# A streaming encoder step: queries projected in transposed form, keys and values two tiles to a PSUM bank

## The reference, cut to what matters

```python
h = rms_norm(x, norm_mix_g)
z = h @ w_in
u_pool, q, k, v, gate_logits = jnp.split(z, IN_SPLITS, axis=-1)
q = rope_partial(q.reshape(B, T, N_HEADS, 2, HEAD_DIM), pos)   # rotates the first 16 of each 64 dims
k = rope_partial(k.reshape(B, T, N_HEADS, 2, HEAD_DIM), pos)
...
s = jnp.einsum('bqhmd,bkhmd->bhmqk', q, k) * ATTN_SCALE        # m: the two halves of a head
p = softmax(where(mask, s, -inf));  a = p[:, :, 0] - lam * p[:, :, 1]
attn = einsum('bhqk,bkhv->bqhv', a, v)
```

## Time and profile before

| | us |
|---|---|
| median of 3 runs | 845.22 |
| lowest, highest | 845.0, 848.85 |
| span of the profiled execution | 843.6 |
| PE busy | 821.1 |
| DVE busy | 588.7 |
| ACT busy | 512.7 |

### The profile page before, as it was taken

One profiled execution on the slowest core, in us unless ns is written; L12 is line 12 of the kernel. 1 busy time (PEld: TensorE's weight loads), 2 busy tenths in 40 slices (PEclk: granted clock), 3 DMA queues, 4 the chain that ended last, 5 costly groups with the idle time before them and its releaser, 6 DMA issues.

```text
span 843.6 us, 15839 instructions
## 1 busy us (share of the span) xinstructions
PE 821.1 (97%) x5378; PEld 748.1 (89%) x5378; DVE 588.7 (70%) x957; ACT 512.7 (61%) x935; POOL 87.6 (10%) x76
## 2 busy tenths in 40 slices
PE   8999999999999999999999999999999999999992
PEld 7999999999999999999999888888888888888881
DVE  6373332777677768467467126999989999989995
ACT  7343313666566656565525233488888887888884
POOL 0000000000000000000000001222223322223112
PEclk9999999999999999999999999999999999999996
DMA  9632213232133213332234746699999999999925
GB/s 274 139 103 83 67 44 95 82 109 75 36 104 107 59 54 108 102 101 75 79 123 157 270 177 204 236 371 372 380 377 374 368 368 367 364 368 367 351 70 193
DMA packets 135959, 163.54 MB, mean 194 GB/s; under 512 B 18599, under 2 KB 103719, under 8 KB 135914
## 3 DMA queue, kind: packets, MB, share of 16 engines
q1 hardware_dynamic: 129674, 149.53, 52.7%
q0 software_dynamic: 5952, 12.82, 5.4%
q10 hardware_dynamic: 288, 0.59, 0.2%
HBM read 151.61 MB, written 20.12 MB: 204 GB/s over the span
## 4 chain that ended last, share of the span: by engine, by line
PE 52%; DVE 3%; DMA 2%; issue 1%; ACT 1%; POOLq 0%; POOL 0%; ACTq 0%
PE ps L1748 15%; PE ps L1750 15%; PE ps L1749 15%; PE ps L2182 2%; PE ps L2094 1%; DMA xg<-sum_rows,idi 1%; PE ps L2101 1%; PE ps L2204 1%; DMA sum_rows<-yb,ydn 1%; PE ps L2086 0%; PE ps L2127 0%; PE ps L2128 0%; PE ps L2025 0%; DVE wl L1144 0%; PE ps L1953 0%
## 5 line engine op out<-in xcount | busy, mean ns | idle before, releaser
L1623 DVE TENSOR_TENSOR wl<-rawM,wh 128x1024 fp32r<-128x1024 f32 x189 | 223.9, 1220 | 14.3 <-ACT wh L980 12.4
L980 ACT ACTIVATE wh<-rawM 128x1024 fp32r<-128x1024 f32 x192 | 195.8, 1057 | 6.2 <-PE ps L1750 2.8
L1748 PE MATMUL ps<-hTh,wh 128*128 128x272 f32 (+2 forms) x448 | 131.0, 292 | 1.4 <-ACT qkv L804 1.0
L1750 PE MATMUL ps<-hTh,wl 128*128 128x272 f32 (+2 forms) x448 | 129.5, 289 | 0.0
L1749 PE MATMUL ps<-hTl,wh 128*128 128x272 f32 (+2 forms) x448 | 128.9, 288 | 0.0
L1748 PE MATMUL ps<-wh,xh 128*128 128x256 f32 (+1 forms) x384 | 124.3, 324 | 0.3 <-DVE xl L1669 0.3
L1750 PE MATMUL ps<-wh,xl 128*128 128x256 f32 (+1 forms) x384 | 121.7, 317 | 0.0
L1749 PE MATMUL ps<-wl,xh 128*128 128x256 f32 (+1 forms) x384 | 121.6, 317 | 0.0
L1748 PE MATMUL ps<-wh,hTh 128*128 128x384 f32 x256 | 90.0, 352 | 0.2 <-DVE mA L1254 0.2
L1748 PEld LDWEIGHTS ps<-hTh,wh 128*128 128x128 f32 x448 | 84.3, 188 | 3.0 <-ACT qkv L804 1.3
L1750 PE MATMUL ps<-wh,hTl 128*128 128x384 f32 x256 | 86.3, 337 | 0.0
(11 more groups left out here) (324 smaller groups left out, 1711.5 us busy)
## 6 DMA issues: line engine op xcount, KB each, us to landing
rawM<-in_w_expert_up SPq DMA_DIRECT2D x64, 512.0 KB, 9.2
rawM<-in_w_expert_down SPq DMA_DIRECT2D x64, 512.0 KB, 8.0
rawM<-in_w_expert_gate SPq DMA_DIRECT2D x64, 512.0 KB
rawA<-in_w_in SPq DMA_DIRECT2D x64, 192.0 KB, 3.0
rawA<-in_w_in SPq DMA_DIRECT2D x20, 512.0 KB, 5.3
rawA<-in_w_attn_branch SPq DMA_DIRECT2D x8, 512.0 KB, 3.5
rawA<-in_w_out SPq DMA_DIRECT2D x8, 512.0 KB, 4.2
x<-in_x_prompt SPq DMA_DIRECT2D x4, 512.0 KB, 6.7
```

What stands on the lines that cost most here:

```text
L980: nc.scalar.activation(wh[:, (c + 1) % S, :], rawM[:, slot, :], ACT.Copy).then_inc(m_hi, 1)
L1623: V.tensor_tensor(wl[:, sl, :], rawM[:, slot, :], wh[:, sl, :].bitcast(F32), ALU.subtract).then_inc(m_lo, 1)
L1748: T.matmul(out, sh, mh_, start=start, stop=False, **kw)
L1750: return T.matmul(out, sl, mh_, start=False, stop=stop, **kw)
```

## The change

Queries leave the token-row form. In each step they are now made by `queries(j, half, ...)`: 128 columns of weights are the stationary operand, and 272 tokens move past, twice, into banks 3 and 4: 6 matmuls of 272 columns. The result is transposed already. Keys and values (`keys_values`) keep the tile as stationary operand, with 256 columns moving; two tiles share a bank, so banks 0, 1 and 2 hold them. In steps 0 to 6 the queries come after the tiles and after the attention pieces that are tied to tile 4, in step 7 ahead of the tiles. `turn(g)` has 6 transposes instead of 11.

ACT copies three key and value banks (512, 512, 256 elements) and then, behind them, the queries (544 elements, `copy_queries`). The rotation of the queries is done in the transposed form by DVE: times a table of signed sines (`scale_queries`), times a table of cosines and a swap of partitions by STREAM_SHUFFLE (`swap_queries`), and an addition (`turn_queries`). They stand at three places of DVE's order. Then ACT rounds them (`qh`) and DVE takes `ql`, each in one instruction of 544. The key rotation is half as wide, and is moved ahead of the second query step. `clamp(g, 0)` is moved behind the splits of q and k; the split of v is behind it. The two tables (128 x 544 each) are loaded once, ahead of the first cached keys.

```diff
+            def copy_queries(h):
+
+                act.wait_ge(q_mm, h + 1)
+                if not (isinstance(h, int) and h == 0):
+                    act.wait_ge(tr_lo, 2 * h)
+                nc.scalar.activation(q_turned[:].rearrange("p (h n) -> p h n", h=2), ps[:, 3:5, 0:HALF],
+                                     ACT.Copy).then_inc(q_ev, 1)
+
+            def evacuate(h, banks=range(NEV)):
+
+                for b in banks:
+                    if b < 2:
+                        act.wait_ge(acc_mm, 2 * h + b + 1)
                     else:
                         act.wait_ge(mm_done, H0 + 4 * h + 4)
-                    if t == 0 and not (isinstance(h, int) and h == 0):
+                    if b == 0 and not (isinstance(h, int) and h == 0):
                         act.wait_ge(kv_out, 64 * h)
                         act.wait_ge(tr_lo, 2 * h)
                         act.wait_ge(vlo_done, h)
-                    nc.scalar.activation(qkv[:, t, :], ps[:, t, 0:384], ACT.Copy).then_inc(acc_ev, 1)
+                    n = len(KV_TILES[b])
+                    nc.scalar.activation(kv[:, 2 * b:2 * b + n, :], ps[:, b, 0:KV * n].rearrange("p (t c) -> p t c", t=n),
+                                         ACT.Copy).then_inc(acc_ev, 1)
 
...
-                dve.wait_ge(acc_ev, NT * (g + 1))
-                V.tensor_tensor(qkv[LAST:P, 4, :], ps[2 * DEC:LAST, 4, 0:384], qkv[LAST:P, 4, :],
+                dve.wait_ge(acc_ev, NEV * (g + 1))
+                V.tensor_tensor(kv[LAST:P, 4, :], ps[2 * DEC:LAST, 2, 0:KV], kv[LAST:P, 4, :],
                                 ALU.add).then_inc(dec_done, 1)
...
+            def scale_queries(g, lk):
+
+                if isinstance(g, int) and g == 0:
+                    dve.wait_ge(qt_in, 32)
+                dve.wait_ge(q_ev, g + 1)
+                lk(V.tensor_tensor(q_swap[:], q_turned[:], q_sin[:], ALU.mult))
+
+            def swap_queries(lk):
+
+                V.tensor_tensor(q_turned[:], q_turned[:], q_cos[:], ALU.mult)
+                lk(V.stream_shuffle(q_swap[:], q_swap[:], HALF_SWAP))
+
+            def turn_queries():
+
+                V.tensor_tensor(q_turned[:], q_turned[:], q_swap[:], ALU.add).then_inc(q_done, 1)
+
             def rope(g, lk):
 
...
 
-                dve.wait_ge(vhi_done, g + 1)
-                V.tensor_tensor(vl[:, 0:NT, :], qkv[:, :, 2 * P:3 * P], vh[:, 0:NT, :].bitcast(F32), ALU.subtract)
-                V.tensor_tensor(vl[:, NT, :], ckv[:, 1, :], vh[:, NT, :].bitcast(F32), ALU.subtract).then_inc(vlo_done, 1)
+                dve.wait_ge(q_hi, g + 1)
+                V.tensor_tensor(ql[:], q_turned[:], qh[:].bitcast(F32), ALU.subtract)
                 dve.wait_ge(tr_hi, 2 * g + 1)
-                V.tensor_tensor(ql[:, 0:SEQ], ps[:, 5, :], qh[:, 0:SEQ].bitcast(F32), ALU.subtract)
                 V.tensor_tensor(kl[:], ps[:, 6, :], kh[:].bitcast(F32), ALU.subtract).then_inc(tr_lo, 1)
                 dve.wait_ge(tr_hi, 2 * g + 2)
-                V.tensor_tensor(ql[:, SEQ:TOK], ps[:, 7, LAST:P], qh[:, SEQ:TOK].bitcast(F32), ALU.subtract)
-                V.tensor_tensor(ktl[:], ps[:, 7, P:3 * P], kth[:].bitcast(F32), ALU.subtract).then_inc(tr_lo, 1)
+                V.tensor_tensor(ktl[:], ps[:, 7, 0:2 * P], kth[:].bitcast(F32), ALU.subtract).then_inc(tr_lo, 1)
+                if not (isinstance(g, int) and g == 0):
+                    clamp(g - 1, 0, lk)
+                dve.wait_ge(vhi_done, g + 1)
+                V.tensor_tensor(vl[:, 0:NT, :], kv[:, :, P:KV], vh[:, 0:NT, :].bitcast(F32), ALU.subtract)
+                V.tensor_tensor(vl[:, NT, :], ckv[:, 1, :], vh[:, NT, :].bitcast(F32), ALU.subtract).then_inc(vlo_done, 1)
                 nxt(3)
                 largest(g, 0, lk)
                 if not (isinstance(g, int) and g == 0):
...
+                rope(h - 1, lk)
+                scale_queries(h - 1, lk)
                 if not first:
                     probs_lo(h - 2, 2)
-                rope(h - 1, lk)
+                swap_queries(lk)
                 lo_head(2, n + 2)
-                if not first:
-                    clamp(h - 2, 0, lk)
+                turn_queries()
                 attend(h - 1, lambda k: lo_head(k % 4, n + k, WH if k == 3 else w_next), lk)
                 assert links[0] == (d1 if first else per_head)
...
 
+            def queries(j, half, sl, q0):
+
+                tc = slice(HALF * half, HALF * (half + 1))
+                return three(ps[:, 3 + half, 0:HALF], wh[:, sl, q0:q0 + P], wl[:, sl, q0:q0 + P], hTh[:, j, tc], hTl[:, j, tc],
+                             j == 0, j == KD - 1)
+
+            def keys_values(j, t, sl, q0):
+
+                wc, first = slice(q0 + P, q0 + 3 * P), j == 0 and t % 2 == 0
+                if t < 4:
+                    return three(kv_bank(t), hTh[:, j, col(t)], hTl[:, j, col(t)], wh[:, sl, wc], wl[:, sl, wc],
+                                 first, j == KD - 1, skip_group_check=True)
+                both = dec[:, 2 * DEC * j:2 * DEC * j + P]
+                T.matmul(kv_bank(t), both, wh[:, sl, wc], start=first, stop=False)
+                return T.matmul(kv_bank(t), both, wl[:, sl, wc], start=False, stop=j == KD - 1)
+
             def project_first():
 
...
                 ins.then_inc(mm_done, 1)
 
             def project(h, j, after={}):
 
                 n = H0 + 4 * h + j // 2
-                sl, k = (H0 + j // 2) % S, j % 2
-                if k == 0:
+                sl, q0 = (H0 + j // 2) % S, 384 * (j % 2)
+                if j % 2 == 0:
                     pe.wait_ge(lo_done, n + 1)
-                wc = slice(384 * k, 384 * k + 384)
+                if j == KD - 1:
+                    queries(j, 0, sl, q0)
+                    queries(j, 1, sl, q0).then_inc(q_mm, 1)
                 for t in range(NT):
-                    if j == 0:
-                        pe.wait_ge(acc_ev, NT * (h - 1) + t + 1)
+                    if j == 0 and t % 2 == 0:
+                        pe.wait_ge(acc_ev, NEV * (h - 1) + t // 2 + 1)
                         if t == 4:
                             pe.wait_ge(dec_done, h)
-                    if t < 4:
-                        ins = three(ps[:, t, 0:384], hTh[:, j, col(t)], hTl[:, j, col(t)], wh[:, sl, wc], wl[:, sl, wc],
-                                    j == 0, j == KD - 1)
-                    else:
-                        both = dec[:, 2 * DEC * j:2 * DEC * j + P]
-                        T.matmul(ps[:, t, 0:384], both, wh[:, sl, wc], start=j == 0, stop=False)
-                        ins = T.matmul(ps[:, t, 0:384], both, wl[:, sl, wc], start=False, stop=j == KD - 1)
-                    if j == KD - 1 and t < 4:
+                    ins = keys_values(j, t, sl, q0)
+                    if j == KD - 1 and t in (1, 3):
                         ins.then_inc(acc_mm, 1)
-                    if t == NT - 1 and k == 1:
+                    if j == KD - 1 and t == NT - 1:
                         ins.then_inc(mm_done, 1)
                     if t in after:
                         after[t]()
+                if j < KD - 1:
+                    if j == 0:
+                        pe.wait_ge(q_ev, h)
+                    queries(j, 0, sl, q0)
+                    ins = queries(j, 1, sl, q0)
+                    if j % 2:
+                        ins.then_inc(mm_done, 1)
 
             def turn(g):
 
                 pe.wait_ge(rope_done, g + 1)
                 if not (isinstance(g, int) and g == 0):
...
             def gate_block(b, after={}):
 
-                if b < 2:
-                    pe.wait_ge(acc_ev, NT * (HEADS - 1) + 2 * b + 2)
+                if b == 0:
+                    pe.wait_ge(acc_ev, NEV * (HEADS - 1) + 2)
+                elif b == 1:
+                    pe.wait_ge(acc_ev, NEV * HEADS)
+                    pe.wait_ge(dec_done, HEADS)
+                    pe.wait_ge(q_ev, HEADS)
```

More of the change, by code:

```diff
@@ L309, in build @@
         eps_added = sem("eps_added")
-        fy_in = [sem(f"fy_in{i}") for i in range(NT)]
+        SUMS_IN = [32] * 4 + [48]
         f_out, f_rt, f_done = (sem(n) for n in ("f_out", "f_root", "f_done"))
@@ L721, in mean_square @@
             def mean_square(t):
[L722 removed]
+                act.wait_ge(rows_in[t], 16 if t < 4 else 32)
                 root(every, t, sq[:, t % 2, :], rt_done)
@@ L911, in head @@
                        early=lambda: evacuate(h, (0,)))
-                evacuate(h, range(1, NT))
+                evacuate(h, range(1, NEV))
+                copy_queries(h)
             head(1)
@@ L1871, in project_first @@
                 for j in range(2):
-                    tile(j, NT - 1)
+                    queries(j, 1, sl, 384 * j)
+                pe.wait_ge(pa_half, 1)
                 for t in range(4):
-                    if t == 0:
-                        pe.wait_ge(pa_half, 1)
-                    if t == 2:
-                        pe.wait_ge(ws_dve, len(dve_jobs))
                     for j in range(2):
-                        ins = tile(j, t)
```

(6 more changed lines are left out.)

112 lines of the change are left out of this document (60 added, 52 removed).

## The result

| | before | changed |
|---|---|---|
| median, us | 845.78 | 854.44 |
| lowest, highest | 845.0, 848.85 | 853.87, 855.86 |
| span of the profiled execution | 843.6 | 854.1 |

The account below looks back on a forecast made before the run. PE was taken as the bound with little room, ACT only 0.14 us ahead at the head boundary. Work -8.7, boundary waits +7.8, scores +3.9, first gate block +0.85 make +3.9 on 845.2: 849.1 us, range 843.5 to 853.5.

Parts of the forecast that it names:

- PE's own work: Matmul steps and transposes on PE: 4.4 us less in 64 steps, 4.3 less in transposes, 8.7 us in all.
- Rival (d): 256-column matmuls limited by weight load: at 0.118 each, 1.8 us of saving lost, about 850; chance 0.55 together with forecast.
- The transposes: Five fewer transposes per head at 0.108 us each: 0.54 us less per head, 4.3 us in 8 heads.
- The head boundary: PE waits 0.7 us before group 1's values and 0.65 before group 2's transposes: 7.8 us over 6 boundaries.
- the first gate block: At the end of the heads, PE waits longer for the copies of head 7: 0.85 us more.
- The scores of group 1: DVE's longer chain delays ACT's exponentials, so PE waits 0.65 us before these scores: 3.9 us in 6 heads.
- the shuffle: In DVE's chain before the largest scores, one pass over 544 elements taken at 0.72 us, 1.45 as upper end.
- the 6 heads whose DVE order is the full one: The only heads given the 0.65 us wait before the scores of group 1, 3.9 us together.
- The attention of head 7 between gate blocks ... fits: PE has over 5 us of work between its pieces there, so DVE's added 1.2 us costs nothing.
- The sum of a steady head: Steady heads would stand 29.4 us apart instead of 28.5.
- (b): Rival of a dearer DVE chain: shuffle at 1.45 us, each steady head 0.7 longer, 853.6 us; chance 0.13.

Follow-up runs that it names:

- q7_last: The changed kernel with the queries of step 7 behind its tiles and the third key and value bank released on its own: 851.59 us, ratio 1.0062.
- qcopy_late: The changed kernel with ACT's copy of the queries behind the output copies of group 1 instead of ahead of them: 854.21 us, ratio 1.0092.
- ath_first: The changed kernel with ACT rounding the probabilities of group 1 before its early copy of the first key and value bank: 856.62 us, ratio 1.0125.
- four_moves: The changed kernel with `add_first`, `q7_last`, `qcopy_late` and head 7's query rounding ahead of the copy of gate block 1: 844.39 us, ratio 0.9985.
- five_moves: `four_moves` with DVE's large split of v also moved behind the largest scores of group 0, the cached rows' split staying: 841.71 us, ratio 0.9945.
- extra_pass: The changed kernel with one more DVE pass of 544 elements behind the low part of the queries, its result unread: 860.88 us, ratio 1.0173.
- before_extra_behind: The kernel before with one more DVE pass of 512 elements behind the splits of q and k, its result unread: 846.06 us, ratio 0.9998.
- add_first: The changed kernel with the addition that ends the query rotation ahead of DVE's weight split instead of behind it: 851.12 us, ratio 1.0056.
- v_late: The changed kernel with both DVE splits of v moved behind the largest scores of group 0: 861.14 us, ratio 1.0171.

## Why the prediction was wrong, point by point

**PE's own work: term mis-sized.** I took 0.116 for a matmul of 256 columns, "the middle" of rows in the experts, and a step of 2.377 us. Five fifth tiles of the changed kernel, four steps without anything between them:

```profile
127.10 0.28 PE L1926 MATMUL ps<-wh,dec 128*128 128x256 f32 x1
...
136.85 0.28 PE L1926 MATMUL ps<-wh,dec 128*128 128x256 f32 x1
```

9.75 / 4 = 2.438 us, with 0.120 per matmul of 256 and 0.126 per one of 272. That is head 0. In the steady heads PE goes a little faster: behind the scores of group 0 the changed kernel has 24 matmuls of 256 columns and 6 of 272 in 3.60 us, the kernel before 24 of 384 in 4.19:

```profile
238.49 0.28 PE L1804 MATMUL ps<-wl,hTh 128*128 128x256 f32 x1
...
242.09 0.28 PE L1805 MATMUL ps<-wh,hTl 128*128 128x256 f32 x1
```

```profile
236.03 0.34 PE L1749 MATMUL ps<-wl,hTh 128*128 128x384 f32 x1
...
240.22 0.34 PE L1750 MATMUL ps<-wh,hTl 128*128 128x384 f32 x1
```

With 0.1255 for 272 columns this is 0.1186 for 256, against 0.1746 for 384: a step of 2.413 us, 0.03 less than before, 0.25 in a head. So 64 steps gave some 1.8 us instead of 4.4. Rival (d) had the size nearly right (0.118, 2.6 us left of the saving). The rows on record held the better value: 0.1746 at 384 and 0.1255 at 272 make a line of 0.44 ns per column, on which 256 costs 0.1185. I had averaged two stages instead of interpolating in my own terms. The transposes gave their 0.5 per head.

**The head boundary: right.** Predicted waits 0.7 and 0.65, 1.35 together; measured 0.57, 0.30 and 0.30, 1.17. Predicted starts of values and transposes X + 2.4 and X + 5.3, measured X + 2.22 and X + 5.23: the chain to the values was 0.18 shorter than worked out. The mechanism (ACT's chain, not PE's work, sets the start) is what `q7_last`, `qcopy_late` and `ath_first` show. At the first gate block 0.85 was predicted; the wait went from 1.17 to 1.77, 0.60.

**The scores of group 1: mechanism right, size off.** PE came at X + 17.96 (predicted X + 18.0), the exponentials ended at X + 18.86 (X + 18.6), and they started 0.14 later: 1.04 instead of 0.65. As 0.09 stands before these scores in the kernel before too, the increase is 0.95, 0.30 over the forecast, in six heads 1.8 us. The largest scores came at X + 15.60 instead of X + 15.35. The term that was too small, by 0.15 of these 0.25, is the shuffle with what follows it: it takes 0.77 us, and its successor starts 0.90 after it (`wl` at 233.00), against 0.75 in the sum. Only 0.05 of that is the shuffle's length; the other 0.10 stands where the loop has a register instruction for the split's wait count between the two (in head 7, outside the loop, the split starts 0.03 after the shuffle's end, here 0.13). The Trainium skill ("VectorE: DVE Perf Modes", The perf-mode tier table) led to an estimate of 0.64; the trace is dearer, and the trace decides.

**The first head: left out.** I gave this wait to "the 6 heads whose DVE order is the full one". But head 1 waits too, 0.30 before the scores of group 0 and 0.49 before those of group 1, 0.6 us more than the 0.09 at each.

**"The attention of head 7 between gate blocks ... fits": this step failed.** It looked at PE's work between the scores and not at who stands behind DVE's chain there. That is a weight split, which gate block 2 needs in its middle, directly behind the scores of group 0. PE, after, then before:

```profile
365.66 0.34 PE L2002 MATMUL ps<-kl,qh 64*128 64x384 f32 x2
367.33 0.40 PE L1803 MATMUL ps<-hTh,wh 128*128 128x272 f32 x1 [1.34 <-DVE wl L1178]
```

```profile
358.50 0.34 PE L1935 MATMUL ps<-kl,qh 64*128 64x384 f32 x2
358.96 0.39 PE L1748 MATMUL ps<-hTh,wh 128*128 128x272 f32 x1
```

and what held DVE up, ACT and DVE after:

```profile
361.29 0.62 ACT L924 ACTIVATE gate<-ps 128x544 f32<-128x544 f32 x1 [0.94 <-PE ps L1805]
361.81 0.65 ACT L877 ACTIVATE qh<-q_turned 128x544 fp32r<-128x544 f32 x1
```

```profile
362.49 0.72 DVE L1384 TENSOR_TENSOR ql<-q_turned,qh 128x544 fp32r<-128x544 f32 x1 [3.56 <-ACT qh L877]
...
366.06 1.22 DVE L1178 TENSOR_TENSOR wl<-rawA,wh 128x1024 fp32r<-128x1024 f32 x1
```

The rotated queries lay ready for over 2 us, but ACT's rounding stands behind its copy of gate block 1. The step from the last scores of group 0 to the next matmul went from 0.46 to 1.67 us, 1.2 more. By order alone `four_moves` brings the step down to 0.98, and in `five_moves` no wait is left there. That the place has no slack for DVE is shown from both sides: `extra_pass` makes the step 2.31, and in the kernel before `before_extra_behind` makes it 1.05 instead of 0.46.

**The sum of a steady head.** Predicted -0.54 (steps), -0.54 (transposes), +1.3, +0.65: +0.87. Measured -0.25, -0.54, +1.15 (1.17 less 0.02 that stood there), +0.95, and -0.07 for the wait before the scores of group 0 that the change removed and I hadn't counted. That makes +1.24; the traces show +1.23.

**What the miss is made of.** Up to the experts it is 8.4 us instead of 3.9, 4.5 more. The steps account for +2.6, the scores of group 1 for +1.8, the gate block of head 7 for +1.2 and the first head for +0.6; the boundaries (-1.0), the scores of group 0 (-0.4) and the first gate block (-0.25) came out cheaper than forecast. So the largest failed term is PE's own work, and the one that was put at nothing is the attention of head 7.

**The range** left out a dearer chain together with cheaper work that doesn't come: (b) and (d) were priced one at a time, and nothing in the prediction ties the one to the other. What came was (d) nearly at its price, and a dearer chain without the dear shuffle of (b): it takes 0.77 us and not over 1.

## What to carry to other kernels

Ask of slack at each place where another engine waits, not of an engine: one more pass on DVE cost 4.5 us in one place of the kernel before and next to nothing three instructions later. When a step is moved, follow every count that it raises, through to what stands behind the waiting transfer in its queue: a split of 0.28 us that moved along or stayed made some 11 us that way. And when a better layout comes out slower, look at the order before undoing it: put work that waits for nothing where PE waits, and other work into a round trip between two engines.

## What the runs showed of the hardware

- Matmuls of 384, 272 and 256 columns follow each other every 0.175, 0.126 and 0.119 to 0.120 us: nearly in line. A step has 5216 columns now and had 5376, but six more matmuls, each with some 0.006 us on top of its columns.
- A STREAM_SHUFFLE of 544 elements takes 0.77 us, a product of 544 0.72. An instruction that waits for the shuffle's end starts 0.03 us after it (in `add_first`, and in head 7 of the changed kernel), as behind other instructions that are waited for; one that waits for nothing starts 0.07 before the product in front of it ends.
- The granted clock fell behind some long waits and not behind others. Stretches right after PE was idle for 1.97 us in `extra_pass`, 2.11 in `v_late` and 2.04 in `ath_first` (stretch; its length, busy PE, PEld, DVE, ACT, POOL; granted clock, DMA share, GB/s):

```profile
372.30:375.30 3.00, 3.00 (x13) 3.00 (x14) 2.65 (x10) 1.65 (x7) 0.00 (x0) 0.50 0.52 175
```

```profile
342.90:346.90 4.00, 3.98 (x19) 3.75 (x21) 2.42 (x5) 2.21 (x10) 0.00 (x0) 0.57 0.01 2
```

```profile
348.80:352.80 4.00, 4.00 (x33) 4.00 (x34) 2.78 (x9) 0.66 (x2) 0.00 (x0) 1.00 0.20 56
```

At 0.50 these 3 us hold 13 matmuls, half the work: it is the 1.5 us more than the waits explain in `extra_pass`. That level is 1.2 GHz of 2.4. Why the third wait cost no clock these rows don't tell.
